# Narrow products with the weights as the stationary side, inside the stages around them, in a two-block model on one core

## What is computed

```
# block 1, layer 0: Mamba-2 mixer
zxbcdt = u @ w_in                       # 1024 -> 2048 (z) + 4096 (xbc) + 32 (dt_raw)
xbc = silu(causal_depthwise_conv(xbc))  # x 2048, B 1024, C 1024 columns
dt  = softplus(dt_raw + dt_bias)        # 256 x 32, one step size per head
y   = ssd_chunked_scan(x * dt, dt * (-exp(a_log)), B, C)
out = rmsnorm((y + x * d_skip) * silu(z)) @ w_out
# ... squared-relu MLP, stick-breaking attention, MLP
# block 2: attention with a relative bias beside a gated delta rule
beta  = sigmoid(h @ w_beta)             # 256 x 4
decay = -exp(a_log2) * softplus(h @ w_decay + dt_bias2)   # 256 x 4
# ... convolution of q, k, v, delta rule, 32 routed experts
```

## Time and profile before

| | |
|---|---|
| three runs | 1381.08, 1381.76, 1386.42 us (median 1381.76) |
| profiled execution | 1387.08 us, span of the instructions 1385.3 us |
| mean granted clock of PE | 0.979 |
| busy, share of the span | PE 96%, PEld 84%, DVE 72%, ACT 53%, POOL 9% |

### The profile page before, as it was taken

One profiled execution on the slowest core, in us unless ns is written; L12 is line 12 of the kernel. 1 busy time (PEld: TensorE's weight loads), 2 busy tenths in 40 slices (PEclk: granted clock), 3 DMA queues, 4 the chain that ended last, 5 costly groups with the idle time before them and its releaser, 6 DMA issues.

```text
span 1385.3 us, 19114 instructions
## 1 busy us (share of the span) xinstructions
PE 1334.1 (96%) x8084; PEld 1168.8 (84%) x8084; DVE 990.7 (72%) x1119; ACT 735.1 (53%) x777; POOL 131.0 (9%) x119
## 2 busy tenths in 40 slices
PE   7999999999999999999999899999999999999996
PEld 7999877799998798799998698788878888878885
DVE  6987564767878735867855745646477788888896
ACT  6655763344444546444444355734434577677673
POOL 0002543110001000100000100015200000000000
PEclk9999999999999999999999989999999999999999
DMA  8552224377877542357775254321254699999993
GB/s 331 183 185 94 95 89 158 146 285 286 310 274 294 192 152 92 122 213 273 277 252 195 103 196 149 106 93 61 66 189 157 217 353 352 335 333 346 345 364 119
DMA packets 41768, 290.29 MB, mean 210 GB/s; under 512 B 4653, under 2 KB 5061, under 8 KB 7632
## 3 DMA queue, kind: packets, MB, share of 16 engines
q1 hardware_dynamic: 35712, 252.76, 49.7%
q0 software_dynamic: 5968, 36.27, 7.0%
HBM read 286.90 MB, written 2.11 MB: 209 GB/s over the span
## 4 chain that ended last, share of the span: by engine, by line
PE 85%; DVE 9%; ACT 3%; DMA 1%; issue 1%; POOL 1%; DVEq 0%; SPq 0%; ACTq 0%; POOLq 0%
PE banks L835 24%; PE banks L837 24%; PE banks L836 24%; DVE w_lo L1617 2%; PE banks L1380 2%; PE banks L1483 1%; DMA raw<-weights 1%; ACT w_hi L392 1%; PE banks L987 1%; DVE mod L1856 1%; DVE pre_norm L1771 1%; PE banks L1163 1%; POOL tiny L2388 1%; PE banks L996 1%; PE banks L890 1%
## 5 line engine op out<-in xcount | busy, mean ns | idle before, releaser
L1617 DVE TENSOR_TENSOR w_lo<-raw,w_hi 128x2048 fp32r<-128x2048 f32 x237 | 542.3, 2295 | 120.6 <-ACT w_hi L392 119.4
L392 ACT ACTIVATE w_hi<-raw 128x2048 fp32r<-128x2048 f32 x237 | 449.9, 1909 | 24.8 <-DMA raw<-weights 24.8
L835 PE MATMUL banks<-hT_hi,w_hi 128*128 128x256 f32 x1120 | 323.8, 289 | 3.3 <-DVE w_lo L1648 3.3
L837 PE MATMUL banks<-hT_hi,w_lo 128*128 128x256 f32 x1120 | 320.0, 286 | 0.0
L836 PE MATMUL banks<-hT_lo,w_hi 128*128 128x256 f32 x1120 | 320.0, 286 | 0.0
L835 PEld LDWEIGHTS banks<-hT_hi,w_hi 128*128 128x128 f32 x1120 | 218.1, 195 | 8.2 <-issue 4.9
L836 PEld LDWEIGHTS banks<-hT_lo,w_hi 128*128 128x128 f32 x1120 | 218.1, 195 | 1.4
L837 PEld LDWEIGHTS banks<-hT_hi,w_lo 128*128 128x128 f32 x1120 | 217.7, 194 | 0.0
L835 PE MATMUL banks<-w_hi,act_hi 128*128 128x512 f32 x256 | 100.2, 391 | 0.4 <-DVE act_lo L1827 0.4
L836 PE MATMUL banks<-w_lo,act_hi 128*128 128x512 f32 x256 | 100.0, 391 | 0.0
L837 PE MATMUL banks<-w_hi,act_lo 128*128 128x512 f32 x256 | 99.7, 389 | 0.0
(11 more groups left out here) (417 smaller groups left out, 2184.2 us busy)
## 6 DMA issues: line engine op xcount, KB each, us to landing
raw<-weights SPq DMA_DIRECT2D x238, 1024.0 KB, 4.8
mod_raw<-weights POOLq DMA_DIRECT2D x24, 1024.0 KB, 5.1
ln_gain_bias<-ln_rows POOLq DMA_DIRECT2D x4, 1024.0 KB, 7.0
h<-x SPq DMA_DIRECT2D x2, 512.0 KB, 4.1
h<-x POOLq DMA_DIRECT2D x1, 1024.0 KB, 5.5
rms_gain<-rms_rows POOLq DMA_DIRECT2D x2, 512.0 KB, 6.2
h_rows<-h POOLq DMA_DIRECT2D x1, 1024.0 KB, 4.4
bias_rows<-bias_table POOLq DMA_DIRECT2D x1, 1024.0 KB, 12.4
```

The lines of the kernel that those rows point to most:

```text
L392: A(hi[u % RING][:, :], raw[u % RING][:, :], ACT.Copy).then_inc(S["w_hi_done"], 1)
L835: mm(out, a[0], b[0], start=start, stop=False)
L837: return mm(out, a[1], b[0], start=False, stop=stop)
L1617: tt(lo[u % RING][:, :], raw[u % RING][:, :], hi[u % RING][:, :].bitcast(F32), ALU.subtract).then_inc(S["w_lo_done"], 1)
```

## The change

- `small_rows` takes the place of `small_product` for the step sizes and for beta/decay: the small weights (32 or 8 columns) are stationary, the 256 tokens move, so there are 24 matmuls with a result of 32 or 8 rows by 256 tokens. ACT copies that result to SBUF (`dt_rows`, `beta_rows`), and `small_columns` turns it back with two transposes.
- The product of the step sizes stands behind projection unit 9 (`DT_AFTER`), its transposes behind unit 10; DVE adds the bias behind its split of iteration 10, ACT's part of softplus stands at the end of its iteration 11 and DVE's between convolution and split of iteration 12. In both places ACT loads one table set that holds both exponential and logarithm.
- Behind unit 15 PE goes to the running sums, two groups of transposes, `z_half(0, 0)`, two groups, `z_half(0, 1)`, four groups, `z_half(1, 0)`. The first four groups wait for single convolutions instead of all silus. DVE's split of iteration 15 moves behind its fourth X group.
- In block 2, `small_columns` stands behind unit `qa` 0. DVE's order is as before: gate first, then the table; the bias table's product now ends ahead of the transposes, and the semaphore counts are changed to suit.

The third narrow product (36 router columns) stays as it is. The diff, with the semaphore counts on POOL that follow the renaming cut:

```diff
@@ -151,6 +151,9 @@
+DT_AFTER = 9
+
+
 def unit_half(t, c):
@@ -241,6 +244,7 @@
         ysk = [mem(f"y_skip{b}", 200 + b, [P, T]) for b in range(2)]
+        dt_rows = mem("dt_rows", 200, [32, T])
@@ -312,6 +316,7 @@
+        bg_rows = mem("beta_rows", 194, [8, T])
         lg = mem("logits", 176, [P, TT, 36])
@@ -436,14 +441,19 @@
                 A(xbcT[:, 2 * n:2 * n + 2, :], acc[n % 2][:, :, :], ACT.Silu).then_inc(S["silu_done"], 1)
+                if n == DT_AFTER:
+                    act.wait_ge(S["narrow_mm"], 1)
+                    A(dt_rows[:, :], PS[0:32, 4, 0:T], ACT.Copy).then_inc(S["narrow_sb"], 1)
+                if n == DT_AFTER + 2:
+                    act.preload_act_table_set("natural_log_exp_and_others")
+                    step(A(rr["a_log"], rr["a_log"], ACT.Exp))
+                    softplus(64, ("dt_read", 1, "dt_exp"))
             def z_read(n):
...
-            step(A(rr["a_log"], rr["a_log"], ACT.Exp))
-            softplus(64, ("dt_read", 1, "dt_exp"))
             act.wait_ge(S["small_mm"], 1 + 1)
@@ -641,8 +651,11 @@
+            act.wait_ge(S["narrow_mm"], 2)
+            A(bg_rows[:, :], PS[0:8, 4, 0:T], ACT.Copy).then_inc(S["narrow_sb"], 1)
             act.wait_ge(S["small_read"], 2 + 1)
             A(beta.rearrange("p (t n) -> p t n", t=TT), bg[:, :, 0:4], ACT.Sigmoid).then_inc(S["small_act"], 1)
+            act.preload_act_table_set("natural_log_exp_and_others")
             step(A(rr["a_log2"], rr["a_log2"], ACT.Exp))
@@ -915,9 +928,16 @@
-            def small_product(outs, c0, n):
+            def small_rows(b, c0, n):
+                for k in range(KD):
+                    last = product(PS[0:n, b, 0:T], [s[:, k, c0:c0 + n] for s in (wsh, wsl)], [f(k) for f in hT],
+                                   k == 0, k == KD - 1)
+                return last
+
+            def small_columns(b, rows, n):
                 for t in range(TT):
-                    last = small_tile(outs[t], t, c0, n)
+                    last = pe.transpose(PS[:, b, T + 64 * t:T + 64 * t + n], rows[:, t * P:(t + 1) * P],
+                                        ident[0:n, 0:n])
                 return last
@@ -926,7 +946,7 @@
                 if c == 0:
-                    pe.wait_ge(*(S["conv_done"], 16) if n == 0 else (S["z_done"], max(n - 1, 1)))
+                    pe.wait_ge(*(S["conv_done"], 14) if n == 0 else (S["z_done"], max(n - 1, 1)))
                 last = half_T(at("in", 16 + n), c, hT, PS[:, (1, 7)[n % 2], c * T:(c + 1) * T])
@@ -934,9 +954,12 @@
                 in_unit(n)
-            pe.wait_ge(S["small_lo_done"], 1)
-            small_product([PS[:, 4, 0:32], PS[:, 4, 32:64]], 0, 32).then_inc(S["small_mm"], 1)
-            z_half(0, 0)
+                if n == DT_AFTER:
+                    pe.wait_ge(S["small_lo_done"], 1)
+                    small_rows(4, 0, 32).then_inc(S["narrow_mm"], 1)
+                if n == DT_AFTER + 1:
+                    pe.wait_ge(S["narrow_sb"], 1)
+                    small_columns(4, dt_rows, 32).then_inc(S["small_mm"], 1)
             da = da_all.rearrange("p (t n) -> p t n", t=TT)
@@ -947,19 +970,23 @@
-                wait(pe, S["x_read"], n - 3)
+                pe.wait_ge(*(S["conv_done"], 13 + n) if n < 4 else (S["x_read"], n - 3))
                 t, k = n // 4, 4 * (n % 4)
...
-            pe.wait_ge(S["silu_done"], 16)
-            for n in range(4):
+            pe.wait_ge(S["silu_done"], 8)
+            for n in range(2):
+                x_rows(n)
+            z_half(0, 0)
+            for n in range(2, 4):
                 x_rows(n)
...
             z_half(1, 0)
+            pe.wait_ge(S["silu_done"], 16)
             pe.wait_ge(S["small_read"], 2)
@@ -1236,14 +1263,17 @@
             pe.wait_ge(S["v_read"], 4 + 2)
-            small_product([PS[:, 4, 0:8], PS[:, 4, 8:16]], 32, 8).then_inc(S["small_mm"], 1)
+            small_rows(4, 32, 8).then_inc(S["narrow_mm"], 1)
             pe.wait_ge(S["tab_in"], 32)
-            pe.wait_ge(S["pool_init"], 1 + 1)
+            pe.wait_ge(S["pool_init"], 2 + 1)
             mm(PS[0:H_A, 5, 0:TABLE_W], relb[:, :], tabs[:, 0:TABLE_W], start=True, stop=True
...
                 unit_T(at(("qa", "ka")[n // 2], n % 2), hT, [PS[:, n, c * T:(c + 1) * T] for c in range(2)])
+                if n == 0:
+                    pe.wait_ge(S["narrow_sb"], 2)
+                    small_columns(4, bg_rows, 8).then_inc(S["small_mm"], 1)
             def conv2_half(i):
@@ -1314,7 +1344,7 @@
             last.then_inc(S["small_mm"], 1)
-            pe.wait_ge(S["g_done"], 1)
+            pe.wait_ge(S["da_done"], 2)
             pe.wait_ge(S["att_oT_lo"], SB_PAIRS + 4)
@@ -1665,15 +1695,19 @@
                 last.then_inc(S["conv_done"], 1)
-                split(at("in", n) + AHEAD)
-            dve.wait_ge(S["small_mm"], 1)
-            tt(sx.rearrange("p (t n) -> p t n", t=TT), PS[:, 4, 0:64].rearrange("p (t n) -> p t n", t=TT),
-               rr["dt_bias"].rearrange("p (o n) -> p o n", o=1).to_broadcast([P, TT, 32]), ALU.add
-               ).then_inc(S["dt_read"], 1)
-            softplus(dt_all, 64, S["dt_exp"])
-            stt(da_all.rearrange("p (t n) -> p t n", t=TT), dt_all.rearrange("p (t n) -> p t n", t=TT), -1.0,
-                rr["a_log"].rearrange("p (o n) -> p o n", o=1).to_broadcast([P, TT, 32]), ALU.mult, ALU.mult
-                ).then_inc(S["da_done"], 1)
+                if n == DT_AFTER + 3:
+                    softplus(dt_all, 64, S["dt_exp"])
+                    stt(da_all.rearrange("p (t n) -> p t n", t=TT), dt_all.rearrange("p (t n) -> p t n", t=TT), -1.0,
+                        rr["a_log"].rearrange("p (o n) -> p o n", o=1).to_broadcast([P, TT, 32]), ALU.mult, ALU.mult
+                        ).then_inc(S["da_done"], 1)
+                if n < 15:
+                    split(at("in", n) + AHEAD)
+                if n == DT_AFTER + 1:
+                    dve.wait_ge(S["small_mm"], 1)
+                    tt(sx.rearrange("p (t n) -> p t n", t=TT),
+                       PS[:, 4, T:T + 128].rearrange("p (t n) -> p t n", t=TT)[:, :, 0:32],
+                       rr["dt_bias"].rearrange("p (o n) -> p o n", o=1).to_broadcast([P, TT, 32]), ALU.add
+                       ).then_inc(S["dt_read"], 1)
@@ -1687,6 +1721,8 @@
                    ALU.mult).then_inc(S["x_read"], 1)
+                if n == 3:
+                    split(at("in", 15) + AHEAD)
@@ -1963,8 +1999,9 @@
             plain_splits("zb", 2)
-            dve.wait_ge(S["small_mm"], 2 + 1)
-            dve.tensor_copy(bg, PS[:, 4, 0:16].rearrange("p (t n) -> p t n", t=TT)).then_inc(S["small_read"], 1)
+            dve.wait_ge(S["small_mm"], 3 + 1)
+            dve.tensor_copy(bg, PS[:, 4, T:T + 128].rearrange("p (t n) -> p t n", t=TT)[:, :, 0:8]
+                            ).then_inc(S["small_read"], 1)
             dve.wait_ge(S["small_read"], 2 + 1)
@@ -1972,8 +2009,8 @@
                 rr["a_log2"].rearrange("p (o n) -> p o n", o=1).to_broadcast([P, TT, 4]), ALU.mult, ALU.mult
-                ).then_inc(S["g_done"], 1)
-            dve.wait_ge(S["small_mm"], 3 + 1)
+                ).then_inc(S["da_done"], 1)
+            dve.wait_ge(S["small_mm"], 2 + 1)
             dve.tensor_copy(tabs[0:H_A, TABLE_W:2 * TABLE_W], PS[0:H_A, 5, 0:TABLE_W]).then_inc(S["tab_sb"], 1)
@@ -2397,8 +2434,8 @@
             pool.wait_ge(S["tr_lo"], 4 + 4)
-            pool.memset(mod[:, :, :], 0.0).then_inc(S["mod_zero"], 1)
-            pool.wait_ge(S["mod_zero"], 1)
+            pool.memset(mod[:, :, :], 0.0).then_inc(S["pool_init"], 1)
+            pool.wait_ge(S["pool_init"], 2)
             pool.dma_start(mod[0:1, :, :].rearrange("p a d -> p (a d)"), b_mod).then_inc(S["mod_in"], 16)
```

More of the change, by code:

```diff
@@ L2228, in select @@
                     last.then_inc(S["gather_ready"], 1)
-            dve.wait_ge(S["pool_init"], 2 + 1)
+            dve.wait_ge(S["pool_init"], 3 + 1)
             select(0)
@@ L2414, in _ @@
             pool.memset(relb[32:33, :], 1.0).then_inc(S["pool_init"], 1)
-            pool.wait_ge(S["pool_init"], 1 + 1)
+            pool.wait_ge(S["pool_init"], 2 + 1)
             pool.dma_start(relb[0:32, :], rel_bias).then_inc(S["tab_in"], 16)
@@ L2459, in _ @@
             pool.dma_start(final_row[:, :], rms_rows[:, 2 * D:3 * D].to_broadcast([P, D])).then_inc(S["final_in"], 16)
-            pool.wait_ge(S["pool_init"], 2 + 1)
+            pool.wait_ge(S["pool_init"], 3 + 1)
             rstd_of(12)
```

## The result

| | runs | median | lowest to highest |
|---|---|---|---|
| before, same chip | 15 | 1385.37 us | 1381.08 to 1390.37 |
| after | 15 | 1379.96 us | 1375.76 to 1382.86 |

The ratio is 0.9958, 95% interval 0.9945 to 0.9971: 5.8 us faster, 4.0 to 7.6. That is 0.42%, a gain that the interval separates from nothing, but under the half per cent that the prediction took as its mark. The forecast was 8.3 us. Note that before itself came out at 1385.37 in more runs, 3.6 above the median of the first three: the number 1373.5 and the gain of 8.3 must be judged apart.

The account below looks back on a forecast made before the run. PE was taken as the bound, 85% of the chain of waits. Savings of 2.4 (step sizes, junction) and 7.0 us (beta/decay) made 9.4, taken as 8.4 off the median 1381.76: 1373.5 us, range 1370 to 1380.

Parts of the forecast that it names:

- The matmuls: Step sizes' product: 48 matmuls of 5.28 us become 24 of 2.9 plus 0.2 for transposes, saving 2.2 us.
- The clock at the two places: Full clock expected around both narrow products, saving 1.5 us at the step sizes and 4.8 at beta/decay (3.9 for the median).
- the clock stays: Rival, 0.14: 8 or 32 result columns count as little work, PE still falls to 1.2 GHz; 1377.8 us.
- The waits: Junction from unit 15 to the scan: late DVE and ACT make PE wait 0.7 and 0.6 us, 1.3 lost.
- Place 2: Beta/decay product to end of unit `qa` 0, block 2: 16.7 us become 9.6, 7.0 saved, 2.2 count and 4.8 clock.
- slower: Rival, 0.03: `bias_rows`, behind the gate in block 2, lands over 4 us later than worked out and becomes the bound; 1388.7 us.
- the sum: Whole kernel: 2.4 + 7.0 = 9.4 us off the profiled 1387.1; for the median 8.4 off 1381.76, said as 1373.5.
- place 1: Step sizes' product and junction up to the scan: 2.2 count + 1.5 clock - 1.3 waits = 2.4 us saved.
- Usual executions lose less: Rival, 0.15: before the change, beta/decay loses only 1.5 us to the clock in most executions; 2.4 + 3.7 saved, 1375.7 us.
- The clock falls elsewhere: Rival, 0.12: the half-clock stretch moves to the junction before the scan and costs 1.5 to 3 us there; 1375.6 us.

Follow-up runs that it names:

- place 2 alone: Kernel before with only the beta/decay product in block 2 changed to the new form: 1384.07 us, ratio 0.9995 against before.
- two padded kernels: Full change plus 15 useless narrow matmuls ahead of the beta/decay product, step sizes' product behind unit 9 or 5: 1376.31 and 1376.24 us.

## Why the prediction was right or wrong

**The matmuls: right.** 2.9 us were forecast for 24, 2.77 and 2.85 came; transposes 0.2, 0.24 came.

**The clock at the two places: right.** 1.00 through both. The form of the product brings it down: busy PE, 32 columns moving, half clock at two places in the program. Against the rule of the Trainium skill that the prediction cites, which asks for an idle PE, stand 6.91 of 6.91 us busy; for the new form stand 96 matmuls at 1.00. The rival "the clock stays" falls.

**The waits: right in kind, high in size.** For the fourth transpose group 0.34 instead of 0.7, for X 0.30 instead of 0.6; the junction 14.64 instead of 15.2 us. The last convolution ended 6.05 us after unit 15, 6.5 were forecast. The product behind unit 5 confirms the cause. The step's term was 1.3 us and measured 0.6.

**Place 2: right.** 7.0 forecast, 6.8 in the profiled pair. The copy of the table began at 818.05, 13.8 us after the product, 13.7 forecast, and `bias_rows` releases PE nowhere: the rival "slower" falls.

**The step that failed: the sum.** It took what lies behind each place as unchanged, at nothing and without a reason, and with it assumed that a saving arrives at the end. In the profiled pair 3.9 us did not: stages A and B ran 1.55 and 1.38 us longer at a lower clock, and C 1.00 us longer by a wait that a shifted half-clock stretch brought. Useless matmuls at place 2 that delay PE by 1.77 us took the loss out of the profile, twice as many put it back, and the same number at place 1 left it. That shifting the entry gives or takes the loss is shown for the full change, by forecasts made ahead of the runs; for place 2 alone such forecasts failed, and the groups of entries fit it only afterwards. Nor does each execution of after lose as its profile does: 6 of its 15 runs lie between 1375.8 and 1377.7, the others between 1379.4 and 1382.9, while both its profiles are of the upper group. In the two padded kernels 11 of 12 runs lie under 1378. I read the lower group as executions without the loss, which an entry a few hundredths of a us away would give; none of them was profiled, so that is argued and not shown.

**The second step that failed: one execution for all.** "Usual executions lose less" was right in kind for place 2: 15.3 us three times of five, a saving of 5.1 there and not the 3.7 of that rival. The 6.1 that the sum took for place 2 in the median is near the 5.8 against the mean. At place 1 the opposite holds, 22.6 us on average for 20.64, and 5.0 us saved for the 2.4 of the sum. Against the means the places save 5.0 + 5.8 = 10.8 us, and the stages behind take 5.0 back (258.7 us against a mean of 253.7 in the five profiles whose place 2 is old), which makes 5.8, the measured gain; by before's own three profiles it is 4.0 + 6.2 - 4.5 = 5.7. Because the loss may be absent in part of the executions, this agreement is partly luck.

**"The clock falls elsewhere"** was the right kind of rival and had the wrong place and size: nothing falls at the junction, where 32 transposes and two waits passed at 1.00; the Trainium skill's sentence on transposes (TensorE: Matmul & The Clock Gate, PE-mode transpose), which spoke for it, is not borne out here, though here the transposes stood in short pieces beside z halves, and no run puts many of them alone. The half clock came back 30 us and more behind the second place instead.

**Open:** why place 2 alone gained only 0.7 us (by its interval between 3.3 gained and 2.1 lost) with a place that is 5 to 7 us shorter in the profile. Part is place 1, which took 22.1 to 23.7 us in its executions; the rest isn't explained. Its three profiled executions took 1381.3 to 1383.1 us, while its runs go up to 1387.7: none of the slow ones was profiled.

## What to carry to other kernels

Where few weight columns meet many tokens, make the weights the stationary side: half the matmuls, and here the clock stayed up. But in a kernel whose later stages touch the half clock now and then, a saving ahead is not yet a saving at the end: compare the unchanged stages of both traces before booking it, profile each kernel several times, and try a delay of one or two us ahead of a stage that lost time. Such a delay is tuned to this exact program, and it would have to be tuned again after every edit.

## What the runs showed that was not expected

- A PE that is busy all the time falls to 1.2 GHz behind 128 stationary and 32 moving columns (two positions) or 8 moving columns (place 2), and stays at 2.4 GHz with 8 stationary and 256 moving columns for 11.24 us, with 32 stationary ones for 4.5 us.
- The router's product, which the change leaves in the old form, goes with a fall too: in all 17 profiles a half-clock stretch begins between 0.3 us before and 0.6 us after the end of one of its halves. Turning it round as well is the next thing to try; no run here did.
- 1.8 us of useless matmuls made a 1380 us kernel about 2.5 us faster (0.3 to 4.4); 3.5 us of them, in the one run, did not.
- The same 490 matmuls and waits of stage A took 80.1, 83.1, 84.7 or 86.3 us, nothing between, at granted clocks of 0.98, 0.94, 0.92 and 0.90.
